# Seven half-size products in place of eight for the gate and up projections of a two-layer encoder

## What is computed

```python
def encoder_layer(x, ...):
    ...
    h = rmsnorm(x, norm_ffn)
    ff = jax.nn.silu(h @ w_gate) * (h @ w_up)
    return x + ff @ w_down
```

## Time and profile before

| | before |
|---|---|
| device time of the runs | 1303.5, 1305.23, 1303.95 us; median 1303.95 |
| span of the profiled execution | 1301.7 us |
| gate/up stage, layer 0 and layer 1 | 250.0 and 242.3 us |
| TensorE busy in the span | 97% |

### The profile page before, as it was taken

One profiled execution on the slowest core, in us unless ns is written; L12 is line 12 of the kernel. 1 busy time (PEld: TensorE's weight loads), 2 busy tenths in 40 slices (PEclk: granted clock), 3 DMA queues, 4 the chain that ended last, 5 costly groups with the idle time before them and its releaser, 6 DMA issues.

```text
span 1301.7 us, 18238 instructions
## 1 busy us (share of the span) xinstructions
PE 1265.2 (97%) x7648; PEld 1022.1 (79%) x7648; DVE 427.5 (33%) x585; ACT 530.4 (41%) x884; POOL 667.3 (51%) x395
## 2 busy tenths in 40 slices
PE   5989999999999999999999999999999999999997
PEld 4657877888888778888877777788888888888885
DVE  5865667632022220000058466663500000000003
ACT  5756655443222222211156766553522222222113
POOL 2664752564555545544436676347355555554441
PEclk9999999999999999999999999999999999999999
DMA  6221212232333223333322211222233333233322
GB/s 222 82 65 50 65 52 65 72 106 101 97 97 97 82 91 98 112 104 97 97 65 82 66 51 65 67 65 84 79 97 97 97 97 97 97 114 97 97 97 81
DMA packets 31186, 115.46 MB, mean 89 GB/s; under 512 B 3456, under 2 KB 3712, under 8 KB 30720
## 3 DMA queue, kind: packets, MB, share of 16 engines
q1 hardware_dynamic: 31104, 114.29, 27.4%
HBM read 112.18 MB, written 2.10 MB: 88 GB/s over the span
## 4 chain that ended last, share of the span: by engine, by line
PE 87%; DVE 6%; ACT 2%; issue 1%; POOL 1%; DMA 1%; SPq 0%; POOLq 0%; DVEq 0%; ACTq 0%
PE ps L1207 18%; PE ps L1209 18%; PE ps L1208 18%; PE ps L1226 6%; PE ps L1229 6%; PE ps L1227 6%; PE ps L1437 2%; PE ps L1423 2%; PE ps L1223 2%; PE ps L1218 2%; PE ps L1220 2%; POOL w_lo L779 1%; DMA w_raw<-in_units 1%; PE ps L1297 1%; PE ps L1385 1%
## 5 line engine op out<-in xcount | busy, mean ns | idle before, releaser
L779 POOL TENSOR_TENSOR w_lo<-w_raw,w_hi 128x1024 fp32r<-128x1024 f32 x192 | 465.5, 2425 | 462.1 <-ACT w_hi L447 388.7
L1207 PE MATMUL ps<-h_hi,w_hi 128*128 128x512 f32 (+1 forms) x1064 | 427.6, 402 | 2.7 <-POOL w_lo L779 1.1
L1209 PE MATMUL ps<-h_hi,w_lo 128*128 128x512 f32 (+1 forms) x1064 | 414.0, 389 | 0.0
L1208 PE MATMUL ps<-h_lo,w_hi 128*128 128x512 f32 (+1 forms) x1064 | 413.4, 389 | 0.0
L447 ACT ACTIVATE w_hi<-w_raw 128x1024 fp32r<-128x1024 f32 x192 | 201.9, 1052 | 200.7 <-PE ps L1229 194.5
L1207 PEld LDWEIGHTS ps<-h_hi,w_hi 128*128 128x128 f32 x1064 | 200.6, 189 | 54.9 <-issue 11.2
L1208 PEld LDWEIGHTS ps<-h_lo,w_hi 128*128 128x128 f32 x1064 | 200.7, 189 | 43.0 <-issue 4.3
L1209 PEld LDWEIGHTS ps<-h_hi,w_lo 128*128 128x128 f32 x1064 | 200.4, 188 | 42.2
L1181 DVE TENSOR_TENSOR hid<-ps,sg 128x512 f32<-128x512 f32 x44 | 30.4, 692 | 421.4 <-PE ps L1209 421.4
L846 POOL TENSOR_TENSOR hid_lo<-hid,hid_hi 128x512 fp32r<-128x512 f32 x44 | 56.8, 1292 | 125.9 <-ACT hid_hi L757 125.9
L757 ACT ACTIVATE hid_hi<-hid 128x512 fp32r<-128x512 f32 x44 | 27.8, 632 | 203.3 <-DVE hid L1181 203.3
(11 more groups left out here) (184 smaller groups left out, 1487.8 us busy)
## 6 DMA issues: line engine op xcount, KB each, us to landing
w_raw<-in_units SPq DMA_DIRECT2D x198, 512.0 KB, 3.6
gain<-in_gain SPq DMA_DIRECT2D x5, 512.0 KB, 4.4
par<-in_par SPq DMA_DIRECT2D x2, 1118.5 KB, 9.0
x<-in_x SPq DMA_DIRECT2D x4, 512.0 KB, 7.5
out_y<-x SPq DMA_DIRECT2D x4, 512.0 KB, 2.6
cst<-in_cst SPq DMA_DIRECT2D x1, 1024.0 KB, 13.2
...
```

Source lines behind the costliest of these rows:

```text
L779: nc.gpsimd.tensor_tensor(w_tile(g, 1), w_raw[:, g % RAW], w_tile(g, 0).bitcast(F32), ALU.subtract).then_inc(s_lo, 1)
L1207: nc.tensor.matmul(out, hi, act_hi, start=start, stop=False)
L1208: nc.tensor.matmul(out, hi, act_lo, start=False, stop=False)
L1209: return nc.tensor.matmul(out, lo, act_hi, start=False, stop=stop)
```

## The change

For a pair p of tiles (gate p, up p) the four products of half the contraction (4 chunks) by half the tokens (one sequence of 256) for gate and the four for up are replaced by seven products m1 to m7 of sums of blocks. The sums of the weight blocks are formed by VectorE in PSUM (`outer_sums`, `fourth_sum`), sums of h once per layer (`first_sums`, `last_sum`), and each product is 4 chunks x 3 passes = 12 matmuls of 256 tokens.

The products of a pair are added in PSUM one onto the other, as a running sum in one half of a bank (`chain`): m1, then m6, m7 and m4 on top. Between them other engines take the sum so far: ScalarE copies it out (copy_m1, copy_u2, copy_u3) or takes silu of it in place (silu_second), VectorE adds it to what m2, m5 or m3 left in another place (gate_first, up_second, up_first) and multiplies (hidden_second, and the second instruction of up_first).

The weights of a pair are loaded in two halves of 512 KB, `load_half`, into rooms of four blocks of 512 columns. Every factor of a product is an item of 512 columns: ScalarE rounds it (`hi_item`); the rest is formed by VectorE for m5, m6, m7 and m4 (their sums are in PSUM) and by GpSimd for m1, m2 and m3 (`lo_item`). The ring holds 6 items. hid is stored in fp32; its rounding and rest are done for f = 0..3 in the stage and for f = 4..21 between the units of the down stage. The filters of layer 1 are computed one way and one bank at a time (`filter_way`, `window_way`), the multiplication and sums of `window_way` in VectorE's queue between the rest of m4(p) and outer_sums(p+1), as are the two `reduce_turn`.

```diff
+OPENING = (("m1", 0), ("m2", 0), ("m1", 1), ("m2", 1), ("m1", 2), ("m2", 2), ("m6", 0), ("m5", 0), ("m6", 1), ("m7", 0),
+           ("m7", 1), ("m4", 0), ("m3", 0), ("m4", 1), ("m5", 1), ("m6", 2), ("m3", 1))
+EARLY = 2
+ITEMS = OPENING + tuple((m, p + d) for p in range(EARLY, FT)
+                        for m, d in (("m6", 0), ("m5", 0), ("m7", 0), ("m1", 1), ("m2", 1), ("m4", 0), ("m3", 0))
+                        if p + d < FT and (m, p + d) != OPENING[-2])
+N_ITEMS = len(ITEMS)
+NUMBER = {item: j for j, item in enumerate(ITEMS)}
+ASIDE_ITEMS = 4
+SUMS = ("m5", "m6", "m7", "m4")
...
+def rest_on_vector(j):
+    m, p = ITEMS[j]
+    return j < ASIDE_ITEMS or (m in SUMS and p >= EARLY)
...
+            def product(L, j):
+                m, p = ITEMS[j]
+                pe.wait_ge(rest_sem(j).sem, rest_sem(j).at(L, REST_RANK[j]))
+                if m == "m1":
+                    if p == 0:
+                        pe.wait_ge(flo.sem, flo.at(L, 3))
+                    elif p >= 3:
+                        pe.wait_ge(hid2d.sem, hid2d.at(L, chain_before(p) + 1))
+                    out, start = chain(p), True
...
+                elif m == "m6":
+                    if p == 0:
+                        pe.wait_ge(slo_v.sem, slo_v.at(L, 2))
+                    pe.wait_ge(gate1.sem, gate1.at(L, p + 1))
+                    out, start = chain(p), False
+                elif m == "m7":
+                    if p == 0:
+                        pe.wait_ge(slo_p.sem, slo_p.at(L, 2))
+                    pe.wait_ge(u2c.sem, u2c.at(L, p + 1))
+                    out, start = chain(p), False
+                elif m == "m4":
+                    if p == 0:
+                        pe.wait_ge(slo_v.sem, slo_v.at(L, 6))
+                    pe.wait_ge(u3c.sem, u3c.at(L, p + 1))
+                    out, start = chain(p), False
+                elif m == "m5":
+                    if p == 0:
+                        pe.wait_ge(slo_v.sem, slo_v.at(L, 4))
+                    if fourth_before(p) is not None:
+                        pe.wait_ge(hid1d.sem, hid1d.at(L, fourth_before(p) + 1))
+                    out, start = fourth(p), True
+                else:
+                    if p == 0:
+                        pe.wait_ge(slo_p.sem, slo_p.at(L, 4))
+                    pe.wait_ge(up2d.sem, up2d.at(L, p + 1))
+                    out, start = fourth(p), False
+                hi, lo = item_tile(L, j, 0), item_tile(L, j, 1)
+                for k in range(KT // 2):
+                    cols = slice(P * k, P * k + P)
+                    nc.tensor.matmul(out, hi[:, cols], factor[m][0][:, k], start=start and k == 0, stop=False,
+                                     skip_group_check=True)
+                    nc.tensor.matmul(out, hi[:, cols], factor[m][1][:, k], start=False, stop=False, skip_group_check=True)
+                    last = nc.tensor.matmul(out, lo[:, cols], factor[m][0][:, k], start=False, stop=k == KT // 2 - 1,
+                                            skip_group_check=True)
+                last.then_inc(prod_done.sem, 1)
...
+            def outer_sums(L, p):
+                raw = raws[raw_room(p)]
+                for n in range(2):
+                    v.wait_ge(s_half[raw_room(p), n], half_value(L, p))
+                if p == EARLY:
+                    v.wait_ge(slo_v.sem, slo_v.at(L, 6))
+                else:
+                    v.wait_ge(item_lo_v.sem, item_lo_v.at(L, REST_RANK[NUMBER["m4", p - 1]]))
+                nc.vector.tensor_tensor(ps[:, 0:2, :], raw[:, 1:3], raw[:, 0:2], ALU.subtract).then_inc(t13.sem, 1)
+                v.wait_ge(t13.sem, t13.at(L, p + 1))
+                nc.vector.tensor_tensor(ps[:, 6, :], raw[:, 2], ps[:, 0, :], ALU.subtract).then_inc(t2.sem, 1)
+            def fourth_sum(L, p):
+                v.wait_ge(item_lo_v.sem, item_lo_v.at(L, REST_RANK[NUMBER["m5", p]]))
+                nc.vector.tensor_tensor(ps[:, 0, :], raws[raw_room(p)][:, 3], ps[:, 6, :], ALU.subtract).then_inc(t4.sem, 1)
+            def gate_first(L, p):
+                v.wait_ge(prod_done.sem, prod_done.at(L, NUMBER["m2", p] + 1))
+                v.wait_ge(m1c.sem, m1c.at(L, p + 1))
+                nc.vector.tensor_tensor(silu[:, p % 3], direct(p), m1_of[:, p % 3], ALU.add).then_inc(gate1.sem, 1)
...
+                lo_item(L, 0)
+                lo_item(L, 1)
+                early_sums(L, 0)
+                lo_item(L, 2)
+                lo_item(L, 3)
+                early_sums(L, 1)
+                norm_ffn(L)
+                for p in range(EARLY, FT):
+                    up_first(L, p - 1)
+                    lo_item(L, NUMBER["m4", p])
                     if L + 1 < DEPTH:
-                        if f == F_NET1:
+                        if p == F_NET1 + 1:
                             v.wait_ge(s_par, 16 * (L + 2))
                             reduce_turn(L + 1, 0, FFN_HY, net_bank(L + 1, 0), C_B1, C_F1)
-                        if f == F_NET2:
+                        if p == F_NET2 + 1:
                             reduce_turn(L + 1, 1, P, net_bank(L + 1, 1), C_B2, C_F2)
-                        if f == F_NET2 + 1:
+                        if p == F_NET2 + 2:
                             hidden_pair(L + 1)
-                        if f == F_W3A:
-                            window(L + 1, 0, 0)
-                            window(L + 1, 0, 1)
-                        if f == F_W3B:
-                            window(L + 1, 1, 0)
-                            window(L + 1, 1, 1)
+                        if p - 1 in F_WAYS:
+                            window_way(L + 1, *F_WAYS[p - 1])
+                    if p + 1 < FT:
+                        outer_sums(L, p + 1)
+                        lo_item(L, NUMBER["m6", p + 1])
+                    up_second(L, p)
+                    if p + 1 < FT:
+                        lo_item(L, NUMBER["m5", p + 1])
+                        fourth_sum(L, p + 1)
+                        lo_item(L, NUMBER["m7", p + 1])
+                    if p + 1 < FT:
+                        gate_first(L, p + 1)
+                    hidden_second(L, p)
+                up_first(L, FT - 1)
...
+                norm_ffn(L)
+                for p in range(EARLY, FT):
+                    copy_u2(L, p)
+                    hi_item(L, NUMBER["m4", p])
+                    hi_item(L, NUMBER["m3", p])
+                    if p + 1 < FT:
+                        hi_item(L, NUMBER["m6", p + 1])
+                    copy_u3(L, p)
+                    if p + 1 < FT:
+                        hi_item(L, NUMBER["m5", p + 1])
+                        hi_item(L, NUMBER["m7", p + 1])
+                        copy_m1(L, p + 1)
+                    if L + 1 < DEPTH and p == F_NET1 + 1:
+                        sine_of(L + 1, 0, hid1, FFN_HY)
+                    if L + 1 < DEPTH and p == F_NET2 + 1:
+                        sine_of(L + 1, 1, hid_a, P)
+                    if p + 2 < FT:
+                        hi_item(L, NUMBER["m1", p + 2])
+                    if p + 1 < FT:
+                        silu_first(L, p + 1)
+                    if p + 2 < FT:
+                        hi_item(L, NUMBER["m2", p + 2])
+                    silu_second(L, p)
...
+                hi_unit(L * UNITS + U_DOWN)
+                hi_unit(L * UNITS + U_DOWN + 1)
                 for f in range(FT - 2):
                     hi_unit(L * UNITS + U_DOWN + f + 2)
+                    if f + 4 < FT:
+                        hid_round(L, f + 4)
...
+def pack_pairs(a, L):
+    gate, up = (a[k][L].reshape(2, KT // 2, P, FT, P).transpose(3, 0, 2, 1, 4).reshape(FT, 2, P, -1) for k in ("w_gate", "w_up"))
+    return np.stack([np.concatenate([gate[:, 0], up[:, 0]], axis=-1), np.concatenate([up[:, 1], gate[:, 1]], axis=-1)], axis=1)
```

More of the change, by code:

```diff
@@ L52 @@
 START_BANKS = ((0, 1), (2, 3), (6, 7), (4, 5))
-FREE_BANKS = (0, 1, 6, 7)
 LEVELS = (128, 64, 32, 16, 8, 4, 2, 1)
@@ L743, in _ @@
                 round_tile(L, 7)
[L744 to L762 removed]
+                hi_unit(L * UNITS + U_OUT + 5)
@@ new lines, in last_rows_rest, with norm_ffn @@
+            def last_rows_rest(L, tt, done):
+                v.wait_ge(shi.sem, shi.at(L, done))
+                nc.vector.tensor_tensor(h_lo[:, 4:8, tok(tt)], ps[:, OUT_BANKS[tt][1], :].rearrange("p (k t) -> p k t", k=4),
+                                        h_hi[:, 4:8, tok(tt)].bitcast(F32), ALU.subtract).then_inc(slo_v.sem, 1)
+            def norm_ffn(L):
+                b = 2 * L + 1
+                for tt in range(TT):
+                    x_add(b, tt)
+                    x_mean(b, tt)
+                    if tt >= 2:
+                        x_rest(b, tt - 2, 1)
+                    x_scale(b, tt)
+                    if 0 < tt < TT - 1:
+                        x_rest(b, tt - 1, 0)
+                first_sums(L, 2)
+                last_sum(L, 2)
+                gate_first(L, 0)
+                first_sums(L, 3)
+                sum_rest(L, 2, 3, 1, s2_raw)
```

(33 more changed lines are left out.)

521 lines of the change are left out of this document (415 added, 106 removed).

## The result

The changed kernel takes **1309.39 us** (median, 1307.64 to 1310.16), the kernel before 1303.95 (1303.5 to 1305.23): ratio 1.0039, 95% interval 1.0029 to 1.005. It is slower by 0.4%; I had forecast 1296.5 and a gain.

What follows compares the result with a forecast made beforehand. TensorE's instruction stream was taken to bound the kernel, priced with waits on a busier VectorE. Layer 1 -6.3 and layer 0 -1.2 took the span from 1301.7 to 1294.2; plus 2.3, 1296.5 us, range 1284 to 1317.

Steps and rivals of the forecast that it cites:

- the period of 10.35: Gate/up stage: m6 to m6 of successive pairs takes 10.35 us, as GpSimd holds up outer_sums; products need 10.04.
- layer 1's stage with the wait behind it: Layer 1's gate/up stage, including the wait on the first down unit: 236.0 us against 242.3, so -6.3.
- the end: Start of the down stage: TensorE does four matmuls, then waits 1.8 us for the first down unit's rest.
- (a): Rival: GpSimd and VectorE do not collide at outer_sums, TensorE's 10.04 rules; about 1284 us; chance 0.14.
- (b): Rival: VectorE and ScalarE instructions cost full duration, period 10.9, kernel slower at 1317 us; chance 0.22.
- (c): Rival: the opening costs twice the forecast as VectorE and GpSimd instructions meet, +11.8, 1308 us; chance 0.10.
- the opening: Start of each gate/up stage: m6(0) 2.5 late, m5(0) 0.95, m4(0) 1.75; with small ones 5.9 us a layer.
- The later of the two: Layer 0's filter periods: each costs the larger of VectorE's and TensorE's extra time, 7.9 us for nine products.
- about 0.3 a piece: Layer 0's filter matmuls on TensorE: about 0.3 us each, lengthening its side by 0.6 or 1.2.
- covered: In each period m4(p) does not wait for copy_u3: done at 7.15 us, m4 starts at 7.24.
- The first reduce_turn: Layer 0: seven VectorE instructions, 2.9 us, of which the wait for GpSimd covers 0.7; adds 2.2.
- The networks: Layer 0: the networks' own matmuls on TensorE add 0.5 us in all.

Runs made afterwards that it cites:

- e1: Changed kernel, with GpSimd's rest of m3(p) waiting until VectorE's first outer sum of pair p+1 is written: 1296.49 us.
- e2: Changed kernel, with ScalarE copying u3 before it rounds the next pair's m6: 1304.77 us.
- e5: Kernel before, with way 1's filter matmuls and the skip row reading the same 64 partitions as way 0: 1310.63 us.
- e4: Changed kernel with the edits of e1, e2 and e3 together: 1293.18 us.
- e3: Changed kernel, with a way's filter matmuls moved from behind m3(p) to behind m2(p+1), ahead of m4(p): 1305.43 us.

## Why the prediction was wrong

**Right.** Spacing 0.12; the period of 10.35 and its cause (10.37; e1 takes the cause away), though half of the loss shows at m4; layer 1's stage with the wait behind it (236.0, measured 235.9); m6(0) 2.4 late for 2.5; the second reduce_turn (2.27 for 2.2); the end, if smaller, 1.2 for 1.8. Of the rivals, (a) is e1: it needed one wait more to come true, and layer 1 then gained 5.1 where I had 5.9. (b) and (c) did not come: the plain period is 10.37, and the opening is as forecast. That 1309.4 lies in the range, near the 1308 of (c), is chance; no rival has the filters' term in it.

The size of the opening (5.9 a layer; measured 5.8 and 6.0, from m1(0) to m6(2) less 15 products and the transposes) is in part luck. Where the clock did not fall, in layer 0 of e2, the waits were 2.4, 0.7 and 1.1 us ahead of m6(0), m5(0) and m4(0), for 2.5, 0.95 and 1.75, and the opening was 0.4 shorter; the fall, which the forecast does not have, made up the rest.

**The step that failed** is layer 0's filters: "The later of the two for the nine products m6(11) to m6(19)", 7.9 us, measured 15.3. Two things were wrong in it.

1. The price: "about 0.3 a piece" was read off, where two ways ran on the two halves of the array at once. One at a time a piece is 0.43 plus about 0.29 per way (e5, e4): 10.9 us for TensorE's side instead of 6.0, and with the restart 1.25 and 2.11 a way. TensorE's side, less its slack of 0.29, is then 0.96 or 1.82. Put into my own rule, the later of the two, this gives 0.96, 1.82, 1.2, 0.96, 1.2, 1.82, 1.2, 0.96, 1.2 = 11.3 instead of 7.9. So the price is 3.4 of the 7.4 missing.
2. "The later of the two": VectorE's extra work delays the rounding of m6, behind which ScalarE's copy for m4 stands. My own working had that copy done at 7.15 for a product that starts at 7.24, and called it "covered"; in layer 0 VectorE brings 0.6 (way 0) or 2.3 us (way 1) more. TensorE so waits at m4, and the filter matmuls come after the wait instead of inside it: the costs add. This is the other 4.0. With the matmuls put inside the wait (e3) the nine periods cost 0.94, 1.82, 1.14, 1.02, 1.14, 1.87, 1.14, 1.01, 1.14 = 11.2 over 10.37, or 11.3 over the 10.36 of the changed kernel: the list above, term by term. With the copy moved (e2) they cost 12.7, so the order alone gives back 2.6 of the 4.0.

**The first reduce_turn** (4.38 for 2.2): 1.2 us is the clock behind a wait of 3.08, and about 1.5 is GpSimd holding two small instructions, one of them by a rest of hid that the forecast left out. These overlap with what its slack takes up, and no run parts the one from the other; in e1 and e4, where neither occurs, it costs 2.0, near the 2.2 forecast. **The networks** cost 0.7 more than given: in e4 their matmuls take 0.66 and 0.72 us over the period, each more than the 0.5 that I had for both.

**The rest of the miss.** The span is 11.6 longer than forecast: 9.8 in layer 0's stage, 0.6 ahead of it and 1.2 between and behind the stages. Of these 1.8, 0.6 in each layer is a wait on a rest in the output projection, which the kernel before does not have:

```profile
925.35 0.73 PE L1740 MATMUL ps<-w_lo,mh_hi 128*128 128x512 f32 x2 [0.64 <-POOL w_lo L1114]
```

The other 0.6 is open. The last 1.3 of the 12.9 comes from my reading of what lies around the span. I took the median of all runs less the span of one, 2.3. The runs list a span for each, and a run's time less its own span is 1.8 or 1.9 us in all of them, of every kernel. The profiled execution was the quickest of the five of the changed kernel (1307.64); the median's own span is 1307.6. So 1.8 us of the miss is how far the median lies above the profiled execution, and 0.5 goes the other way.
